# Order of the high and the low product within a block of weights, in a two-layer state-space and two-layer attention model

## What is computed

```python
u = x @ w_in                    # every layer: a wide product of the normed x
...
return y @ w_out
...
x = x + mixed @ w_o[l]
x = x + conv_gated_ffn(rms_norm(x, norm2_g[l]), w_up[l], conv_w[l], conv_b[l], w_down[l])
```

## Time and profile before

| | us |
|---|---|
| median of 3 runs (3503.18 to 3504.74) | 3503.55 |
| the profiled execution | 3501.08 |
| its span in the profile | 3499.3 |

### The profile page before, as it was taken

The page is one execution under the profiler, slowest core; times in us unless marked ns, Lnnn a source line. Parts: engine busy times, 40 slices in busy tenths (PEclk is TensorE's granted clock), DMA queues, the critical chain, the costliest instruction groups (busy, mean ns, idle before and its releaser), DMA issues.

```text
span 3499.3 us, 52970 instructions
## 1 busy us (share of the span) xinstructions
PE 3435.5 (98%) x19584; PEld 2974.8 (85%) x19584; DVE 2730.6 (78%) x3931; ACT 1896.0 (54%) x2906; POOL 1733.5 (50%) x1473
## 2 busy tenths in 40 slices
PE   8999999999999999999999999999999999999999
PEld 7888888888887888888888888888888888888888
DVE  8769887679899966788888658877688888668874
ACT  6555885455555654765544434444765544444443
POOL 4325772278888822153666306652153666206640
PEclk9999999999999999999999999999999999999999
DMA  5554556555555556544555665566544555665566
GB/s 191 171 163 155 173 180 186 188 192 184 180 175 180 171 174 188 182 144 141 187 187 187 185 189 188 187 184 188 181 145 144 186 186 188 183 191 187 187 184 178
DMA packets 177041, 624.38 MB, mean 178 GB/s; under 512 B 19784, under 2 KB 25616, under 8 KB 175760
## 3 DMA queue, kind: packets, MB, share of 16 engines
q1 hardware_dynamic: 171216, 606.11, 55.0%
q10 hardware_dynamic: 5568, 14.89, 1.1%
HBM read 618.75 MB, written 2.17 MB: 177 GB/s over the span
## 4 chain that ended last, share of the span: by engine, by line
PE 80%; DVE 10%; issue 4%; ACT 3%; POOL 3%; DMA 0%; ACTq 0%; SPq 0%; POOLq 0%; DVEq 0%
PE psG L535 47%; PE psG L533 26%; DVE WL L1284 3%; PE psG L532 3%; ACT WH L776 1%; ACT L796 1%; DVE Et L1577 1%; DVE sdx L1297 1%; PE psM L558 1%; POOL SQ L1766 1%; POOL GV L1916 1%; DVE sds L1326 0%; DVE sdx L1589 0%; DVE sds L1313 0%; DVE Y L1289 0%
## 5 line engine op out<-in xcount | busy, mean ns | idle before, releaser
L535 PE MATMUL psG<-H,WH 128*128 128x512 f32 x5655 | 2017.3, 397 | 0.0
L1284 DVE TENSOR_TENSOR WL<-RAW,WH 128x1024 fp32r<-128x1024 f32 (+1 forms) x1162 | 1521.3, 1309 | 484.5 <-ACT WH L776 482.3
L776 ACT ACTIVATE WH<-RAW 128x1024 fp32r<-128x1024 f32 (+1 forms) x1162 | 1214.3, 1045 | 875.0 <-PE psG L535 856.2
L533 PE MATMUL psG<-H,WL 128*128 128x256 f32 x6032 | 1654.9, 285 | 3.8 <-DVE WL L1284 3.8
L535 PEld LDWEIGHTS psG<-H,WH 128*128 128x128 f32 x5655 | 1065.3, 188 | 235.3
L533 PEld LDWEIGHTS psG<-H,WL 128*128 128x128 f32 x6032 | 1141.9, 189 | 42.8 <-issue 4.8
L535 PE MATMUL psG<-Y,WH 128*128 128x512 f32 x2792 | 987.8, 397 | 0.0
L533 PE MATMUL psG<-Y,WL 128*128 128x256 f32 x2944 | 801.6, 281 | 1.0 <-DVE Y L1289 1.0
L535 PEld LDWEIGHTS psG<-Y,WH 128*128 128x128 f32 x2792 | 524.2, 188 | 119.2
L533 PEld LDWEIGHTS psG<-Y,WL 128*128 128x128 f32 x2944 | 555.3, 189 | 15.3 <-DVE Y L1289 1.3
L1925 POOL TENSOR_SCALAR fou<-fsu,PAR 128x256 f32<-128x256 f32 x88 | 177.9, 2022 | 564.7 <-DVE fsu L1326 564.7
(11 more groups left out here) (360 smaller groups left out, 3534.3 us busy)
## 6 DMA issues: line engine op xcount, KB each, us to landing
RAW<-in_w_up SPq DMA_DIRECT2D x352, 512.0 KB, 3.7
RAW<-in_w_o_in SPq DMA_DIRECT2D x162, 512.0 KB, 3.7
RAW<-in_w_e_in SPq DMA_DIRECT2D x128, 512.0 KB, 3.6
RAW<-in_w_down SPq DMA_DIRECT2D x128, 512.0 KB, 3.5
RAW<-in_w_in SPq DMA_DIRECT2D x112, 512.0 KB, 3.6
RAW<-in_w_o SPq DMA_DIRECT2D x72, 512.0 KB, 3.6
RAW<-in_w_e_out SPq DMA_DIRECT2D x64, 512.0 KB, 4.3
RAW<-in_w_o_out SPq DMA_DIRECT2D x64, 512.0 KB, 4.1
```

The costliest lines, as they stand in the source:

```text
L533: ins = e.matmul(o[:, 0:T], wl, x[:, 0:T], start=False, stop=False, skip_group_check=True)
L535: ins = e.matmul(o, wh, x, start=False, stop=last)
L776: copy = lambda o, i, scale=1.0: e.activation(o, i, ACT.Copy, scale=scale)
L1284: tt(WL_[c % NRAW][:, 0:n], RAW_[c % NRAW][:, 0:n], WH_[c % NW][:, 0:n].bitcast(F32), SUB).then_inc(sem("wl"), 1)
```

## The change

In `blocks`, the high product now comes first in every block, and the low one second. The products are the same, with the same operands and the same waits. The flag that opens the accumulation stays on the high product of a tile's first block, and the flag that closes it moves to the low product of the last block, which now also raises `big`.

```diff
-                if k == 0:
-                    e.matmul(o, wh, x, start=True, stop=False)
-                ins = e.matmul(o[:, 0:T], wl, x[:, 0:T], start=False, stop=False, skip_group_check=True)
-                if k > 0:
-                    ins = e.matmul(o, wh, x, start=False, stop=last)
+                e.matmul(o, wh, x, start=k == 0, stop=False, skip_group_check=True)
+                ins = e.matmul(o[:, 0:T], wl, x[:, 0:T], start=False, stop=last, skip_group_check=True)
                 if last or n == len(S.chunks[c][2]) - 1:
                     ins.then_inc(sem("big"), 1)
```

## The result

| | before | changed |
|---|---|---|
| median, us | 3503.61 (4 executions, 3503.18 to 3504.74) | 3481.40 (4 executions, 3480.47 to 3485.76) |
| profiled execution, us | 3501.08 | 3480.91 |
| its span, us | 3499.3 | 3479.0 |

The ratio is 0.9939, 95% interval 0.9927 to 0.9952: faster by 22 us, or 0.6%. The forecast was 3475 with a range of 3466 to 3508.

A forecast was written before the change was run, and what follows sets the result against it. The prediction took TensorE, busy 98% of the span, as the bound. From the profiled execution, 3501.1 - 25 - 5 + 1 = 3472 us; with the median 2.5 us above that execution, about 3475 us, range 3466 to 3508.

The forecast's parts named there:

- What bounds the kernel: Whole kernel: TensorE, busy 98% of the span, is the bound; order can act only through the start-to-start distance of products.
- The stretches, -25 us: Two feed-forward stretches of 2112 blocks: both take the quick gait, 346.7 ns a block for 352.6, 12.5 us each.
- Outside, -5 us: The 4944 blocks outside the stretches: a quarter slow where 40% were, -5 us, bounds -13 and +20 us.
- The small products' new neighbour, +1 us: At 276 small products, the weight load is hidden under 256 columns, not 512: 4 ns each, +1 us.
- A seam costs about nothing: Where equal widths meet at 577 removed seams: four products take 0.70 us; under 10 ns saved or lost each.
- Order is nothing: Rival, whole kernel: products cost their own columns and loads, gaits come from something in time; 3503 to 3504 us, chance 0.08.
- The slow gait holds both stretches: Rival: small products opening both feed-forward stretches leave TensorE slow; +3 us there, about 3503 us in all, chance 0.20.
- Slow everywhere: Rival: strict alternation leads into the slow gait at every small product; up to +20 us outside, about 3526 us, chance 0.15.

The follow-up runs named there:

- e1: The kernel before, with the high product first in every block of the up and down projections only; 3478.57 us, ratio 0.9932.
- e4: The changed kernel with 18 single blocks, in the output projections and the first up projection, turned to low product first; 3487.93 us in one execution.
- e3: The changed kernel with the norm's small product just inside each feed-forward part issued twice, same result; 3479.70 us.
- e7: The changed kernel with one more small product, its result unused, at the end of the first tile of each 32-block output projection; 3479.11 us.
- e6: The changed kernel with the low product first in just two of 9168 blocks, one near the start of each up projection; median 3480.25 us.
- e8: The changed kernel itself, measured again on one chip beside the run with added small products; 3478.80 us.
- e11: The changed kernel itself, measured again on one chip beside the runs with products grouped by width or paired; 3480.41 us, ratio 0.9934.
- e2: The kernel before, with the high product first in every block outside the up and down projections only; 3499.96 us, ratio 0.9991.
- e10: The changed kernel with the low product first in every odd block, so that equal widths stand in pairs; 3481.54 us, ratio 0.9943.

## Why the prediction came out right, point by point

The forecast for the median was -29 us from before (-25 - 5 + 1); measured are -22. The stretches and the small products came as forecast, the term outside didn't.

**What bounds the kernel** was right: TensorE is busy throughout both stretches, and its start-to-start distance is what changed there. No other engine's busy time moved by more than 8 us. Outside, TensorE also waits: for `Et` at its costliest wait 20.8 us before and 17.2 now, so that a slower gait ahead of such a wait is in part hidden by it.

**The stretches, -25 us.** Measured -24.6 (744.8 to 732.6 and 744.6 to 732.2). The price, 12.5 us for each, and the mechanism hold; e1 puts the whole of it there, and e4 shows both gaits held over hundreds of blocks of strict alternation. That both would be quick was a bet at 0.45 against the earlier trace rows, and that it came true was luck in so far as the count behind it (95 to 30) says nothing of this product. Split by kind, the kernel before is quick behind 25 of the 30 groups of eight products at line 675 where the gait can be read, and slow behind six of eight lone products of line 516, which is the kind that opens the stretches. Those six include neither of the openers, behind which a seam comes too soon for this count; the earlier trace rows shows the first of them slow. The changed kernel's timeline at the first stretch, where the earlier trace rows left the slow gait:

```profile
1713.30 0.40 PE L531 MATMUL psG<-H,WH 128*128 128x512 f32 x1
1713.53 0.28 PE L532 MATMUL psG<-H,WL 128*128 128x256 f32 x1
1713.65 0.59 PE L516 MATMUL psM<-SS,ONE 128*128 128x256 f32 x2
1713.89 0.59 PE L531 MATMUL psG<-H,WH 128*128 128x512 f32 x1
1714.32 0.28 PE L532 MATMUL psG<-H,WL 128*128 128x256 f32 x1
1714.43 0.39 PE L531 MATMUL psG<-H,WH 128*128 128x512 f32 x1
```

In all nine profiled executions with this order at this place (the changed kernel three times, e1, and e3 to e7, in e3 with the product doubled) both stretches open quick. In e1, e3, e6, e8 and e11 TensorE came out of the attention's output projection slow, ahead of both stretches, and the norm's product turned it quick. So with this neighbourhood the product is no accident but, at least in these eighteen cases, leads to the quick gait from either one. Why its twin ahead of a low product led to the slow one I don't know.

**Outside, -5 us.** This step failed: by the table the other six parts take +3.6 us in the profiled execution, -1.1 in e8 and +3.9 in e11. By the medians on the three chips, less 24.6 us for the stretches, the rest is +2.4, -0.5 and +1.7 us. (e2, with the same order outside, is at -3.2, its interval from -6.3 to 0, so even the sign isn't settled.) I had taken a quarter of the blocks as slow, from a count of places behind which the gait was slow (30 of 125). In the changed kernel the same count gives 66 of 154, since a low product ahead and a high one behind are another neighbourhood, as I had noted and then not priced. Of the blocks outside that stand in undisturbed runs, 53% are slow in its profile, 47% in e8 and 59% in e11, where I had said 25% and before had 40%. The SSD layer has the largest share of the turn (356 slow blocks before, 731 with the change, 846 in e8, 871 in e11). It comes behind its groups of eight small products: before, 25 quick and 5 slow, with the change 6 quick and 24 slow (5 and 26 in e8, 4 and 26 in e11). One of them, before:

```profile
805.57 0.87 PE L675 MATMUL psM<-Et,Xk 128*64 128x256 f32 x8 [0.46 <-DVE Et L1577]
...
806.96 0.39 PE L535 MATMUL psG<-H,WH 128*128 128x512 f32 x1
...
808.00 0.39 PE L535 MATMUL psG<-H,WH 128*128 128x512 f32 x1
```

and the same one in the changed kernel:

```profile
807.50 0.87 PE L672 MATMUL psM<-Et,Xk 128*64 128x256 f32 x8 [0.47 <-DVE Et L1574]
...
808.75 0.40 PE L531 MATMUL psG<-H,WH 128*128 128x512 f32 x1
...
809.81 0.40 PE L531 MATMUL psG<-H,WH 128*128 128x512 f32 x1
```

Three blocks behind it take 1.04 us before and 1.06 with the change. So the change reversed the outcome by the kind of small product: for the better behind the lone products of line 516 (24 quick, 2 slow), for the worse behind these. And the count was of places, where the cost goes by blocks: the two output projections, 1024 blocks together, have few small products, so one outcome decides some 500 blocks. They went slow in both windows shown above and quick in both in e8; before, their seams had flipped the gait at every tile and so halved the loss.

**The small products' new neighbour, +1 us.** Before, a high product, the small one and a low one take 0.78 us (1709.35 to 1710.13 in the earlier trace rows); now a low product, the small one and a high one take 0.79 (1713.53 to 1714.32 above). Summed over all 276 places in the two profiles, the time beyond that of their blocks goes from 255.4 to 256.6 us, waits included: +1.3 us.

**A seam costs about nothing** was right in size: where equal widths stand in pairs throughout (e10), a block costs 348.5 ns, between the gaits. That is 697 ns for a seam's four products, where the earlier trace rows had 0.70 us.

**The rivals.** "Order is nothing" is out by e1, e2 and e4. "The slow gait holds both stretches" did not come, but e4 shows that it can be held through a stretch from some block on, and the upper executions of e6 make it likely for nearly all of one. "Slow everywhere" had a point in the SSD layer, where most groups of small products now lead to the slow gait.

## What to carry to other kernels

Where an engine is the bound and busy all the time, read the distance from start to start in several places and not the mean of a group: here 346.7 and 353.3 ns for the same two products stood side by side in one trace, and the mean of rows (397 and 285 ns) showed neither. Before ordering products for a gain of a few ns, ask what resets the engine's rhythm and how many products lie behind it; with two blocks changed, single executions took up to 28 us more than the median of the same kernel without that change. And a kernel of this kind should be judged over several executions, since the same program may take another gait: so it did in the output projections of the changed kernel.

## What the runs showed of the hardware that I had not expected

- A product of 512 columns in a row of such products holds TensorE for 226.7 ns and one of 256 columns for 120 ns, at the full granted clock, with a weight load each and operands in `fp32r`: 32 cycles of 2.4 GHz above the columns for both.
- Alternating, the pair has two stable spacings, 346.7 and 353.3 ns, each held for hundreds of blocks (2100 at the longest for the quick one, 990 for the slow one in e4), over borders of tiles, waits that are already met, and changes of bank. The quick one has two forms, some 347 ns throughout or 343 and 350 in turn. Grouped by four the block costs 351, in pairs 348.5.
- One block in another order can switch the gait (five of six in the up projection in e4, none of twelve in the output projections), by its position in the three-block rhythm of the slow gait, or by the form of the quick one. What in TensorE has this rhythm stays open; nothing tried here looks inside it.
- The executions of the kernel before lie within 5 us of each other on each chip, those of the changed one within 9 and those of e6 within 32. In the three profiles of the changed kernel the long stretches are alike and the output projections differ (180.1 or 183.3 us, 187.7 or 190.4), so a part of its scatter comes from there. That the seams are what kept the kernel before steadier is likely but not shown, as it has one profile.
